# Rotary keys turned two pages at a time, sequences written out, and the sample states decayed on GpSimd

## The chip, the core and the metric

The kernel runs on one core of a Trainium2 chip. The metric is the device time of one launch in microseconds. The kernel before took 3429.12 us (median of three runs, 3422.21 to 3435.35). The engines are called PE (TensorE; its weight loads are listed as PEld), DVE (VectorE), ACT (ScalarE), POOL (GpSimd) and SP (SyncE, which issues DMAs).

## What is computed

One inference step of a two-layer trunk for a prompt of 256 tokens and for 8 sample sequences of 4 tokens. Each layer projects the normalized input once and feeds three branches, a Mamba-2 SSD, an RWKV-7 mixer and latent attention, merges them through gates, and adds a convolutional feed-forward part. Two pieces matter here.

Attention of the samples over 16 cached pages of 128 positions each. A key is the 128 features made from the latent by a weight, beside 64 rotary features shared by all heads:

```python
kn = jnp.einsum('blr,rhe->blhe', ckv, w_kb)
kp = jnp.broadcast_to(kpe[:, :, None, :], kn.shape[:-1] + (MLA_ROPE,))
k = rmsnorm(jnp.concatenate([kn, kp], axis=-1), k_norm_g)
sc = jnp.einsum('bqhe,blhe->bhql', q, k) * scale     # then a softmax over 2048 + 4 positions
```

The SSD recurrence, over two chunks of 128 for the prompt and one of 4 for each sample, from a given state:

```python
y_diag = einsum('bcgjls,bcsgjp->bclgjp', cb * exp(segsum(da)), xd)
states = einsum('bclgn,bcgjl,bclgjp->bcgjpn', bm, decay_to_end, xd)
h_next = h * exp(cs[..., -1]) + states
y_off  = einsum('bclgn,bcgjpn,bcgjl->bclgjp', cm, h_in, exp(cs))
```

## The kernel before, in words

The layers run in a loop of two turns. Inside, each stage is a block in which every engine has its own instruction list; semaphores order them, and a barrier of all engines closes the stage. The order of the work within an engine is the order in which the code is written; nothing plans it.

**cache_attention** (`def cache_attention`, L1091) works through 8 sequences of 16 pages. For each page PE turns the latents (two 128x128 transposes, L1224) and the rotary keys (one of 128x64, L1225) into `turn_bank`; ACT copies the latents to `ch` with rounding (L1305) and the rotary keys to `kpT` (L1306); DVE makes the rest `cl` (L1374). The keys then take 18 products of 352 columns (L1245: three parts of float32r, two halves of the rank, three bank groups), and one plain float32 product (L1249) adds the scores of the rotary part from 64 rows. ACT squares the keys (L1319), DVE sums them (L1388). While a sequence runs, the softmax and value steps of the one before are spread over its pages by `finish`: TURN_TOP and SPREAD (L1257, L1260) turn and spread the maximum. The turn of page j+1 is queued ahead of the keys of page j. `seqs` (L1152) writes out the first and the last sequence; the six between run in a loop of three turns, two sequences a turn, on PE, ACT and DVE. Beside it POOL runs the recurrence of the RWKV samples. SP issues the page loads.

**mla_absorb** (L963) runs before it and builds `qr`, the rotary part of the queries, with one DVE copy (L1035) that PE waits for, and ends with a chain on DVE and ACT that makes the scores of the new tokens.

**ssd_tiles** (L2518) follows the SSD projection. After the products inside the first prompt chunk (L2600), PE turns the 8 sample states (`turn_state`, L2619: 8 transposes a sequence into one of two bank pairs), ACT copies each to `seq_T` (L2771), and `read_states` (L2626) reads four at a time; `seq_T` has four slots, so the fifth copy waits for the first reading. Then come eight `update(b)` (16 products each, of 32 rows; on the helper's line L2571), the samples' own output (`inside(SAM)`, L2597 and L2603), the turn of the second chunk's x (`turn_x`, L2584), its four `segments` (one product of 512 columns each, L2571), its reading of the prompt state (`yo`), the new prompt state, `inside(1)` (L2600, L2606) and the turn of the prompt state (L2739), which ACT copies (L2776) and SP stores. DVE decays and adds each sample state in `add(b)`, eight instructions (L2826), and SP stores it. PE's list and DVE's list interleave the pieces so that the two bank pairs 0 to 3 and the banks 4 to 7 come free in time. The stage behind it is `merge`, whose first instruction on ACT is L1673.

Of the kernel before, what the change touches and what calls it, by code (L numbers as in the profile page):

```python
# [962 lines left out]
def mla_absorb(nc, k):  # L963


    with Stage(nc) as st:
# [9 lines left out]
        with st.block() as block:  # L976
# [6 lines left out]
            def _(pe):  # L983
# [22 lines left out]
                nc.tensor.matmul(banks[0:NSAM, 7, 0:256], k.kpe_rT[:, SEQ:T], k.qr[:, :, :].rearrange("p b c -> p (b c)"),  # L1006
# [18 lines left out]
            def _(dve):  # L1025
# [9 lines left out]
                nc.vector.tensor_copy(k.qr[:, :, :].rearrange("p b (h t) -> p h b t", h=HEADS),  # L1035
                                      k.qrT[:, :, SEQ:T].rearrange("p h (b t) -> p h b t", b=NB)).then_inc(qa_kept, 1)
# [54 lines left out]
def cache_attention(nc, k):  # L1091
# [19 lines left out]
    with Stage(nc) as st:  # L1111
# [16 lines left out]
        kpT = reuse(1344, 2, P)[0:ROPE, :, :]  # L1128
# [53 lines left out]
        with st.block() as block:  # L1182
# [33 lines left out]
            def _(pe):  # L1216
                def turn(b, slot, uses, j):
# [5 lines left out]
                    for r in range(2):  # L1223
                        nc.tensor.transpose(xbank[:, r * P:(r + 1) * P], lat[:, slot, j, r * P:(r + 1) * P], k.col("ident"))  # L1224
                    nc.tensor.transpose(xbank[0:ROPE, 2 * P:3 * P], kpe[:, slot, j, :], k.col("ident")).then_inc(turned, 1)  # L1225

                def body(b, slot, uses):
                    base = b * PAGES
                    pe.wait_ge(q_split, b + 1)
                    for j in range(PAGES):  # L1230
# [18 lines left out]
                        nc.tensor.matmul(kbank[:, bank, o:o + 32], kpT[:, x, :], k.qr[:, ds(b, 1), :].rearrange("p o c -> p (o c)"),  # L1249
# [40 lines left out]
            def _(act):  # L1290
# [8 lines left out]
                def head(b, j):  # L1299
# [5 lines left out]
                    nc.scalar.copy(ch[:, x, :], xbank[:, 0:2 * P])  # L1305
                    nc.scalar.copy(kpT[:, x, :], xbank[0:ROPE, 2 * P:3 * P]).then_inc(headed, 1)  # L1306
# [1211 lines left out]
def ssd_tiles(nc, k):  # L2518
# [8 lines left out]
    with Stage(nc) as st:  # L2527
# [24 lines left out]
        h_turned, h_kept, yo_made, y_scaled, y_made, y_read, skip_ready = (st.sem(n) for n in (  # L2552
            "state_turned", "state_kept", "y_from_state", "y_state_scaled", "y_made", "y_read", "skip_ready"))
        dcol_ready, c_zero, cm_ready, bm_ready = (st.sem(n) for n in ("skip_column", "c_cleared", "c_masked", "b_masked"))
        up_made, nat_ready, s_out, p_out = (st.sem(n) for n in ("update_made", "state_updated", "sample_states_stored", "prompt_state_stored"))
# [9 lines left out]
        with st.block() as block:  # L2565
            @block.tensor
            def _(pe):
# [42 lines left out]
                def turn_state(b):  # L2610
# [3 lines left out]
                    elif b == 1:  # L2614
                        pe.wait_ge(ssm_kept, 1)
                    else:
                        pe.wait_ge(h_kept, b - 1)
# [4 lines left out]
                def read_states(m):  # L2622
                    pe.wait_ge(h_kept, 4 * m + 4)
# [6 lines left out]
                def update(b):  # L2630
                    if b < 2:
                        pe.wait_ge(h_kept, 7 + b)
# [62 lines left out]
                for b in range(6):  # L2695
                    turn_state(b)
# [10 lines left out]
                pe.wait_ge(y_read, 1)  # L2707
# [4 lines left out]
                pe.wait_ge(steps_in_1, 2)  # L2712
                segments(1, 0, 5)
                update(3)
                pe.wait_ge(y_read, 2)
                segments(1, 1, 4)
                update(4)
                pe.wait_ge(m_exp, 6)
                segments(1, 2, 5)
                update(5)  # L2720
                pe.wait_ge(m_exp, 7)
                segments(1, 3, 4)
                pe.wait_ge(xdd_ready, 3)
                for g in range(2):
                    last = one(banks[:, 6 + g, :], k.xbcT[:, 10 + g, cols[1]], ssm_T[:, g * 512:(g + 1) * 512])
                last.then_inc(yo_made, 1)
                update(6)
                update(7)
                pe.wait_ge(nat_ready, 7)
                for g in range(2):  # L2730
# [301 lines left out]
```

## Time and profile before

| what | us |
|---|---|
| median of three runs | 3429.12 |
| the profiled execution | 3435.03 |
| its span | 3433.2 |
| PE busy (share of the span) | 2973.6 (87%) |
| DVE busy | 1851.0 (54%) |
| ACT busy | 1332.6 (39%) |
| POOL busy | 849.6 (25%) |
| mean granted PE clock | 0.917 |

A profile is one execution; its span is the time from the first instruction to the last, 1.8 us less than the execution's own time. An engine can be busy without being at its peak: matmuls are pipelined and their listed durations overlap, so the distance between two starts tells more than a duration. PEclk 1.00 is 2.4 GHz, 0.50 is 1.2 GHz. Cache attention lies at about 547 to 1080 us of the span in the first layer and at 2250 to 2790 us in the second; the ssd stage at 1181 to 1270 us and at 2884 to 2975 us.

### The profile page before, as it was taken

Reading aid. Unit: us, or ns where it says so; the run is one execution under the profiler, and the core shown is the slowest. Engines: PE = TensorE matmul, PEld = TensorE weight load, DVE = VectorE, ACT = ScalarE, POOL = GpSimd, SP = SyncE. Lnnn points to the kernel's source line nnn. Section 1 sums busy time; section 2 is a strip of 40 time slices with the busy share of each in tenths; the row PEclk is TensorE's granted clock in tenths of the full one; section 3 lists DMA queues with packets and bytes.
Section 4 is the critical chain, followed back from the end, with each engine's and each line's share of the span. In section 5 each row is a group of like instructions: output and inputs, shape, how many; then the busy total and the mean of one; then the engine's idle time right before and its main releaser. Section 6 shows DMA issues by size and latency. Waiting matters only on the chain. (4 is left out here: it accounts for less than half of the span.)

```text
span 3433.2 us, 67647 instructions
## 1 busy us (share of the span) xinstructions
PE 2973.6 (87%) x26688; PEld 2662.5 (78%) x26688; DVE 1851.0 (54%) x3191; ACT 1332.6 (39%) x2096; POOL 849.6 (25%) x688
## 2 busy tenths in 40 slices
PE   7659687999997879989986687789999978799898
PEld 6559546888886759989984685478888867599898
DVE  5563353555554745569455534545555537554793
ACT  3412343444443324344344123434444434233543
POOL 0041000699970100000001310007999501000000
PEclk9879888999998979999988898889999989699999
DMA  5100302211112336455450002021111132453654
GB/s 165 45 2 5 112 6 68 64 32 45 50 56 89 101 93 181 127 148 147 116 168 18 3 15 101 10 69 59 35 54 38 56 114 76 129 161 110 161 143 120
DMA packets 444034, 282.38 MB, mean 82 GB/s; under 512 B 64686, under 2 KB 439256, under 8 KB 443082
## 3 DMA queue, kind: packets, MB, share of 16 engines
q1 hardware_dynamic: 441492, 276.85, 28.5%
q8 instruction: 212, 3.47, 0.4%
q10 hardware_dynamic: 2232, 1.26, 0.2%
q14 instruction: 98, 0.80, 0.1%
HBM read 258.75 MB, written 19.29 MB: 81 GB/s over the span
## 5 line engine op out<-in xcount | busy, mean ns | idle before, releaser
L1245 PE MATMUL key_banks<-w_kb_head,latent_T_head 128*128 128x352 f32 x1536 | 519.0, 338 | 0.0
L1245 PE MATMUL key_banks<-w_kb_rest,latent_T_head 128*128 128x352 f32 x1536 | 496.9, 324 | 0.0
L1245 PE MATMUL key_banks<-w_kb_head,latent_T_rest 128*128 128x352 f32 x1536 | 496.5, 323 | 0.0
L290 DVE TENSOR_TENSOR w_rests<-w_ring,w_heads 128x2048 fp32r<-128x2048 f32 (+1 forms) x180 | 390.0, 2170 | 161.7 <-ACT w_heads L284 161.2
L284 ACT CAST w_heads<-w_ring 128x2048 fp32r<-128x2048 f32 (+1 forms) x180 | 325.6, 1812 | 60.4 <-DMA w_ring<-in_w_in_dram 22.8
L1065 POOL TENSOR_TENSOR rwkv_state_tmp<-rwkv_state,vec 128x1024 f32<-128x1024 f32 x64 | 153.5, 2398 | 681.7 <-DMA rwkv_state<-in_state_rwkv_dram 676.9
L1305 ACT CAST latent_T_head<-turn_bank 128x256 fp32r<-128x256 f32 x256 | 95.5, 373 | 558.4 <-PE turn_bank L1225 558.4
L1388 DVE TENSOR_REDUCE w_kb<-key_sq 128x8 f32<-128x1024 f32 x256 | 309.4, 1209 | 0.0
L1374 DVE TENSOR_TENSOR latent_T_rest<-turn_bank,latent_T_head 128x256 fp32r<-128x256 f32 x256 | 108.6, 424 | 363.3 <-ACT w_kb L1306 363.3
L1245 PEld LDWEIGHTS key_banks<-w_kb_rest,latent_T_head 128*128 128x128 f32 x1536 | 291.2, 190 | 0.0
L1245 PEld LDWEIGHTS key_banks<-w_kb_head,latent_T_head 128*128 128x128 f32 x1536 | 290.7, 189 | 0.1
L1245 PEld LDWEIGHTS key_banks<-w_kb_head,latent_T_rest 128*128 128x128 f32 x1536 | 290.1, 189 | 0.0
L1319 ACT ACTIVATE key_sq<-key_banks 128x1056 f32<-128x1056 f32 x256 | 269.2, 1052 | 8.7 <-PE key_banks L1249 8.7
L297 PE MATMUL ffn_banks<-h_heads_T,w_heads 128*128 128x288 f32 x704 | 211.6, 301 | 25.6 <-DVE h_rests_T L2041 22.3
L406 POOL TENSOR_TENSOR bonus_product<-fT 128x2304 f32<-128x2304 f32 x2 | 10.1, 5042 | 854.7 <-DVE fT L436 854.7
L298 PE MATMUL ffn_banks<-h_rests_T,w_heads 128*128 128x288 f32 x704 | 209.3, 297 | 0.0
L299 PE MATMUL ffn_banks<-h_heads_T,w_rests 128*128 128x288 f32 x704 | 208.6, 296 | 0.0
L1068 POOL TENSOR_TENSOR rwkv_state_tmp<-rwkv_state_tmp 128x512 f32<-128x512 f32 (+4 forms) x320 | 197.1, 616 | 25.1
L297 PEld LDWEIGHTS ffn_banks<-h_heads_T,w_heads 128*128 128x128 f32 x704 | 133.6, 190 | 29.2 <-DVE h_rests_T L2041 23.2
L297 PE MATMUL merge_banks<-out_heads,w_heads 128*128 128x288 f32 x512 | 151.6, 296 | 5.3 <-DVE out_rests L1713 5.3
L299 PE MATMUL merge_banks<-out_heads,w_rests 128*128 128x288 f32 x512 | 151.7, 296 | 0.0
L298 PE MATMUL merge_banks<-out_rests,w_heads 128*128 128x288 f32 x512 | 151.7, 296 | 0.0
(561 smaller groups left out, 7424.6 us busy)
## 6 DMA issues: line engine op xcount, KB each, us to landing
w_ring<-in_w_in_dram SPq DMA_DIRECT2D x48, 1024.0 KB, 5.4
w_ring<-in_ffn_w_up_dram SPq DMA_DIRECT2D x88, 512.0 KB, 4.9
latents<-in_cache_kv_latent_dram SPq DMA_DIRECT2D x256, 128.0 KB, 2.0
w_ring<-in_w_gate_dram SPq DMA_DIRECT2D x48, 512.0 KB, 3.9
w_ring<-in_ffn_w_down_dram SPq DMA_DIRECT2D x32, 384.0 KB, 3.3
w_ring<-in_ffn_w_down_dram SPq DMA_DIRECT2D x32, 320.0 KB, 3.8
rope_keys<-in_cache_k_rope_dram SPq DMA_DIRECT2D x256, 32.0 KB, 1.8
ssm_native<-in_state_ssm_dram SPq DMA_DIRECT2D x16, 512.0 KB, 7.2
```

The costliest lines, as they stand in the source:

```text
L284: nc.scalar.copy(heads[:, slot, 0:tiles * P], ring[:, slot, 0:tiles * P]).then_inc(rounded, 1)
L290: ops.tensor_tensor(rests[:, slot, 0:tiles * P], ring[:, slot, 0:tiles * P], heads[:, slot, 0:tiles * P].bitcast(F32), ALU.subtract).then_ ...
L297: nc.tensor.matmul(out, wh, xh, start=start, stop=False)
L298: nc.tensor.matmul(out, wh, xl, start=False, stop=False)
L299: return nc.tensor.matmul(out, wl, xh, start=False, stop=stop)
L1065: c(nc.gpsimd.tensor_tensor(tmp, S, over_v(n, t), ALU.mult))
L1068: c(nc.gpsimd.tensor_tensor(tmp[:, :, 0:w], tmp[:, :, 0:w], tmp[:, :, w:2 * w], ALU.add))
L1245: last = nc.tensor.matmul(kbank[:, 3 * x + n, 0:KB], c[:, x, r * P:(r + 1) * P], w[:, r, cols], start=r == 0 and m == 0, stop=r == 1 and m ...
L1305: nc.scalar.copy(ch[:, x, :], xbank[:, 0:2 * P])
L1319: nc.scalar.activation(sq[:, x, :], kbank[:, 3 * x:3 * x + 3, 0:KB], ACT.Square).then_inc(squared, 1)
L1374: nc.vector.tensor_tensor(cl[:, x, :], xbank[:, 0:2 * P], ch[:, x, :].bitcast(F32), ALU.subtract).then_inc(t_kept, 1)
L1388: nc.vector.tensor_reduce(ss[:, slot, j, :], sq[:, x, f:f + KW].rearrange("p (h e) -> p h e", e=NOPE), AX.X, ALU.add).then_inc(summed, 1)
```

## The change

In cache attention the rotary keys of an even page and the odd one behind it are turned by one 128x128 transpose, into a `kpT` of 128 rows, and copied once. The product with the queries now runs over all 128 rows for every page, with a `qr` of two halves that holds zeros in the rows of the other page; one copy and two memsets more on DVE build it in mla_absorb. All eight sequences are written out on PE, ACT and DVE; SP keeps its loop. In ssd_tiles the states are turned as before but copied by ACT (even) and DVE (odd); POOL multiplies each whole state by its decay after it is turned; `add(b)` is one DVE addition; the second chunk's x is turned early, its segments and the prompt's pieces are written in another order and in other banks, and the prompt state is turned before `inside(1)`.

```diff
@@ mla_absorb, vector
-                nc.vector.tensor_copy(k.qr[:, :, :].rearrange("p b (h t) -> p h b t", h=HEADS), ...)
+                for half in range(2):
+                    rows = slice(ROPE * half, ROPE * half + ROPE)
+                    last = nc.vector.tensor_copy(k.qr[rows, half, :, :].rearrange("p b (h t) -> p h b t", h=HEADS), ...)
+                last.then_inc(qa_kept, 1)
+                nc.vector.memset(k.qr[ROPE:P, 0, :, :], 0.0)
+                nc.vector.memset(k.qr[0:ROPE, 1, :, :], 0.0)
@@ cache_attention, seqs
-            body(0, 0, 0)
-            with eng.Fori(0, NB // 2 - 1) as i:
-                body(i * 2 + 1, 1, i)
-                body(i * 2 + 2, 0, i + 1)
-            body(LAST, 1, NB // 2 - 1)
+            for b in range(NB):
+                body(b, b % 2, b // 2)
@@ tensor
-                    nc.tensor.transpose(xbank[0:ROPE, 2 * P:3 * P], kpe[:, slot, j, :], k.col("ident")).then_inc(turned, 1)
+                    if j % 2 == 0:
+                        pair = kpe[:, slot, j:j + 2, :].rearrange("p j c -> p (j c)")
+                        nc.tensor.transpose(xbank[:, 2 * P:3 * P], pair, k.col("ident")).then_inc(turned, 1)
+                    else:
+                        last.then_inc(turned, 1)
...
-                        nc.tensor.matmul(kbank[:, bank, o:o + 32], kpT[:, x, :], k.qr[:, ds(b, 1), :]...
+                        nc.tensor.matmul(kbank[:, bank, o:o + 32], kpT[:, j // 2 % 2, :], k.qr[:, x, ds(b, 1), :]...
@@ scalar
-                    nc.scalar.copy(kpT[:, x, :], xbank[0:ROPE, 2 * P:3 * P]).then_inc(headed, 1)
+                    if x == 0:
+                        last = nc.scalar.copy(kpT[:, j // 2 % 2, :], xbank[:, 2 * P:3 * P])
+                    last.then_inc(headed, 1)
@@ ssd_tiles, tensor
-                for b in range(6):
+                turn_state(0)
+                turn_state(1)
+                pe.wait_ge(y_read, 1)
+                turn_x(1, 4)
+                for b in range(2, 6):
                     turn_state(b)
...
                 read_states(1)
+                pe.wait_ge(steps_in_1, 2)
+                pe.wait_ge(xdd_ready, 3)
+                segments(1, 0, 4)
+                segments(1, 1, 5)
                 pe.wait_ge(bm_ready, 1)
                 update(0)
                 update(1)
+                pe.wait_ge(m_exp, 6)
+                segments(1, 2, 4)
+                pe.wait_ge(m_exp, 7)
+                segments(1, 3, 5)
...
-                inside(SAM, 4, True)
-                turn_x(1, 6)
+                inside(SAM, 6, True)
...
@@ scalar
-                for b in range(NB):
+                for b in range(0, NB, 2):
...
@@ gpsimd
+                pool.wait_ge(e_ready, 2)
+                for b in range(NB):
+                    pool.wait_ge(h_turned, b + 1)
+                    nc.gpsimd.tensor_tensor(nat[:, b, :, :], nat[:, b, :, :], bc(dec[:, :, b], P), ALU.mult).then_inc(decayed, 1)
@@ vector
                 def add(b):
                     dve.wait_ge(up_made, b + 1)
-                    for t in range(DT):
-                        last = nc.vector.scalar_tensor_tensor(nat[:, b, t, :], nat[:, b, t, :], dec[:, t, b:b + 1], ...
+                    dve.wait_ge(decayed, b + 1)
...
+                    nc.vector.tensor_tensor(state, made, state, ALU.add).then_inc(nat_ready, 1)
+
+                def keep(b):
+                    dve.wait_ge(h_turned, b + 1)
+                    if b >= 4:
+                        dve.wait_ge(yo_made, 1)
+                    nc.vector.tensor_copy(seq_T[:, b % 4, :], wide(2)).then_inc(odd_kept, 1)
...
-                finish(0, 1)
-                scaled(SAM, 0, 2)
-                dve.wait_ge(e_ready, 2)
+                finish(0, 1, 4)
+                keep(1)
+                dve.wait_ge(x_turned, 3)
+                dve.wait_ge(s_made, 1)
+                weighted(xd[:, 0, :], 4, dt[:, 1, :])
+                weighted(xdd[:, 0, :], 4, dt_end[:, 1, :]).then_inc(xdd_ready, 1)
+                for b in (3, 5, 7):
+                    keep(b)
+                scaled(SAM, 0, 2, 6)
                 add(0)
                 add(1)
...
```

PE's list at the end of page 1 of cache attention, before: the last key products (L1245), the rotary product, the turn of page 3 and the first products of page 2.

```order
L1245 MATMUL key_banks<-w_kb_rest,latent_T_head 128x352
L1245 MATMUL key_banks<-w_kb_head,latent_T_rest 128x352
L1249 MATMUL key_banks<-qr,w_kb 128x32
L1224 MATMUL turn_bank<-const,latents 128x128 x2
L1225 MATMUL turn_bank<-const,rope_keys 64x128
L1245 MATMUL key_banks<-w_kb_head,latent_T_head 128x352
```

The same place in the changed kernel:

```order
L1251 MATMUL key_banks<-w_kb_rest,latent_T_head 128x352
L1251 MATMUL key_banks<-w_kb_head,latent_T_rest 128x352
L1255 MATMUL key_banks<-qr,w_kb 128x32
L1226 MATMUL turn_bank<-const,latents 128x128 x2
L1251 MATMUL key_banks<-w_kb_head,latent_T_head 128x352
L1251 MATMUL key_banks<-w_kb_rest,latent_T_head 128x352
```

The third transpose is gone on every odd page; on even ones it stays, with 128 columns in place of 64.

PE's list in the ssd stage from the products inside the first chunk on, before (`ssm_native` are the sample states, `ssm_T` their turned copies, `b_by_seq` marks the updates, `decay_matrix,const` the segments):

```order
L2600 MATMUL ssd_banks<-decay_matrix,x_dt 64x128 x16
L2619 MATMUL ssd_banks<-const,ssm_native 128x128 x48
L2626 MATMUL ssd_banks<-ssm_T,samT 32x512 x8
L2619 MATMUL ssd_banks<-const,ssm_native 128x128 x16
L2626 MATMUL ssd_banks<-ssm_T,samT 32x512 x8
L2571 MATMUL ssd_banks<-b_by_seq,x_dt_decayed 128x128 x16
```

and in the changed kernel:

```order
L2608 MATMUL ssd_banks<-decay_matrix,x_dt 64x128 x16
L2627 MATMUL ssd_banks<-const,ssm_native 128x128 x16
L2592 MATMUL ssd_banks<-const,xbcT 128x128 x8
L2627 MATMUL ssd_banks<-const,ssm_native 128x128 x32
L2635 MATMUL ssd_banks<-ssm_T,samT 32x512 x8
L2627 MATMUL ssd_banks<-const,ssm_native 128x128 x16
L2635 MATMUL ssd_banks<-ssm_T,samT 32x512 x8
L2579 MATMUL ssd_banks<-decay_matrix,const 128x512 x2
L2579 MATMUL ssd_banks<-b_by_seq,x_dt_decayed 128x128 x16
L2579 MATMUL ssd_banks<-decay_matrix,const 128x512 x2
```

The turn of x stands among the states, and all four segments of the second chunk stand in pairs around the first two updates.

PE's list at the end of the stage, before, from `update(5)` on (`prompt_ssm_T,xbcT` reads the prompt state, `x_dt_decayed,b_tm` makes the new one):

```order
L2571 MATMUL ssd_banks<-b_by_seq,x_dt_decayed 128x128 x8
L2571 MATMUL ssd_banks<-decay_matrix,const 128x512
L2571 MATMUL ssd_banks<-prompt_ssm_T,xbcT 128x512 x2
L2571 MATMUL ssd_banks<-b_by_seq,x_dt_decayed 128x128 x16
L2571 MATMUL ssd_banks<-x_dt_decayed,b_tm 128x512 x2
L2600 MATMUL ssd_banks<-decay_matrix,x_dt 64x128 x2
L2606 MATMUL ssd_banks<-const,ssm_T 128x128
```

and in the changed kernel, from `update(2)` on:

```order
L2579 MATMUL ssd_banks<-b_by_seq,x_dt_decayed 128x128 x16
L2579 MATMUL ssd_banks<-prompt_ssm_T,xbcT 128x512 x2
L2579 MATMUL ssd_banks<-b_by_seq,x_dt_decayed 128x128 x16
L2579 MATMUL ssd_banks<-x_dt_decayed,b_tm 128x512 x2
L2579 MATMUL ssd_banks<-b_by_seq,x_dt_decayed 128x128 x16
L2746 MATMUL ssd_banks<-const,prompt_ssm_T 128x128 x8
L2608 MATMUL ssd_banks<-decay_matrix,x_dt 64x128 x2
L2614 MATMUL ssd_banks<-const,ssm_T 128x128
```

The turn of the prompt state (L2746) has moved ahead of the products inside the chunk, which now end PE's list.

## Rows read from the trace of the kernel before

**Rows 1.** The stretches: length, busy us by engine, PEclk, DMA share, GB/s.

```profile
560.00:580.00 20.00, 20.00 (x127) 18.69 (x126) 9.21 (x17) 8.80 (x18) 0.00 (x0) 1.00 0.32 91
1221.00:1244.00 23.00, 23.00 (x112) 15.20 (x109) 14.61 (x45) 2.39 (x4) 0.00 (x0) 0.50 0.37 115
1245.00:1251.00 6.00, 3.40 (x36) 2.29 (x35) 5.23 (x16) 0.00 (x0) 0.00 (x0) 1.00 0.17 53
```

**Rows 2.** Timeline of weight loads, one page: start us, us, what, idle before.

```profile
706.18 0.29 PEld L1249 LDWEIGHTS key_banks<-qr,w_kb 64*128 64x128 f32 x2 [0.22 <-issue]
706.52 0.20 PEld L1224 LDWEIGHTS turn_bank<-const,latents 128*128 128x128 f32 x2
706.68 0.11 PEld L1225 LDWEIGHTS turn_bank<-const,rope_keys 128*64 128x64 f32 x1
```

**Rows 3.** The same page boundary, ACT and PE.

```profile
702.48 0.40 PE L1260 MATMUL misc_bank<-w_kb,const 32*128 32x32 f32 x2 [0.24 <-ACT w_kb L1344]
703.67 0.26 ACT L1306 COPY w_kb<-turn_bank 64x128 f32<-64x128 f32 x1
```

**Rows 4.** PE, first product of rotary keys of some pages, both layers.

```profile
614.45 0.40 PE L1249 MATMUL key_banks<-qr,w_kb 64*128 x2
1002.75 0.41 PE L1249 MATMUL key_banks<-qr,w_kb 64*128 64x32 f32 x2
1062.91 0.29 PE L1249 MATMUL key_banks<-qr,w_kb 64*128 64x32 f32 x1
2318.89 0.29 PE L1249 MATMUL key_banks<-qr,w_kb 64*128 x1
2706.43 0.41 PE L1249 MATMUL key_banks<-qr,w_kb 64*128 64x32 f32 x2
```

**Rows 5.** DVE in the absorb stage and at the start of the next.

```profile
531.54 0.28 DVE L1035 COPY qr<-qrT 64x256 f32<-64x256 f32 x1
538.28 0.29 DVE L1356 COPY new_c_and_one<-new_c 128x256 f32<-128x256 f32 x1 [1.40 <-PEq L228]
```

**Rows 6.** PE, plain float32 products of 128 and of 64 rows.

```profile
487.69 0.79 PE L858 MATMUL attn_banks<-knT,qnT 128*128 128x128 f32 x2
488.41 0.79 PE L859 MATMUL attn_banks<-krT,qrT 64*128 64x128 f32 x2
489.14 1.22 PE L858 MATMUL attn_banks<-knT,qnT 128*128 128x256 f32 x2
```

**Rows 7.** PE in the ssd stage of the first layer.

```profile
1202.46 1.96 PE L2619 MATMUL ssd_banks<-const,ssm_native 128*128 128x128 f32 x16
1208.92 1.92 PE L2626 MATMUL ssd_banks<-ssm_T,samT 128*32 128x512 f32 x16
1217.07 2.05 PE L2571 MATMUL ssd_banks<-b_by_seq,x_dt_decayed 32*128 32x128 f32 x32
1227.01 2.08 PE L2571 MATMUL ssd_banks<-b_by_seq,x_dt_decayed 32*128 32x128 f32 x16
1229.02 2.08 PE L2571 MATMUL ssd_banks<-decay_matrix,const 128*128 128x512 f32 x2
1252.78 0.70 PE L2600 MATMUL ssd_banks<-decay_matrix,x_dt 128*64 128x128 f32 x4
1263.47 1.91 PE L2739 MATMUL ssd_banks<-const,prompt_ssm_T 128*128 128x128 f32 x8
```

**Rows 8.** The other engines in and behind the ssd stage.

```profile
1190.70 3.75 POOL L2791 TENSOR_TENSOR decay_matrix<-const,dt_a 128x1024 f32<-128x1024 f32 x2
1191.39 1.26 DVE L2855 TENSOR_TENSOR dt_to_end<-dt,exp_sums 128x48 f32<-128x48 f32 x1
1252.95 1.22 DVE L2893 TENSOR_TENSOR prompt_ssm_T<-prompt_ssm_T,ssd_banks 128x1024 f32<-128x1024 f32 x1 [0.60 <-PE ssd_banks L2571]
1265.42 1.01 ACT L2776 COPY x_dt<-ssd_banks 128x1024 f32<-128x1024 f32 x1 [21.65 <-PE ssd_banks L2739]
1270.73 2.22 ACT L1673 ACTIVATE merged<-ssd_yT 128x1152 f32<-128x1152 f32 x2 [4.30 <-PEq L228]
```

More of the change, by code:

```diff
@@ L1005, in _ @@
                                      start=r == 0, stop=False)
[L1006 removed]
+                nc.tensor.matmul(banks[0:NSAM, 7, 0:256], k.kpe_rT[:, SEQ:T], k.qr[0:ROPE, 0, :, :].rearrange("p b c -> p (b c)"),
                                  start=False, stop=True).then_inc(new_made, 1)
@@ L1034, in _ @@
                                           banks[:, 4, r * 256:(r + 1) * 256].rearrange("p (h b t) -> p h b t", h=HEADS, b=NB)).then_inc(qa_kept, 1)
-                nc.vector.tensor_copy(k.qr[:, :, :].rearrange("p b (h t) -> p h b t", h=HEADS),
-                                      k.qrT[:, :, SEQ:T].rearrange("p h (b t) -> p h b t", b=NB)).then_inc(qa_kept, 1)
+                for half in range(2):
+                    rows = slice(ROPE * half, ROPE * half + ROPE)
+                    last = nc.vector.tensor_copy(k.qr[rows, half, :, :].rearrange("p b (h t) -> p h b t", h=HEADS),
+                                                 k.qrT[:, :, SEQ:T].rearrange("p h (b t) -> p h b t", b=NB))
+                last.then_inc(qa_kept, 1)
+                nc.vector.memset(k.qr[ROPE:P, 0, :, :], 0.0)
+                nc.vector.memset(k.qr[0:ROPE, 1, :, :], 0.0)
                 dve.wait_ge(squared, 2)
@@ L1248, in body @@
                         bank, o = score_place(x, slot)
-                        nc.tensor.matmul(kbank[:, bank, o:o + 32], kpT[:, x, :], k.qr[:, ds(b, 1), :].rearrange("p o c -> p (o c)"),
+                        nc.tensor.matmul(kbank[:, bank, o:o + 32], kpT[:, j // 2 % 2, :], k.qr[:, x, ds(b, 1), :].rearrange("p o c -> p (o c)"),
                                          start=False, stop=True, skip_group_check=True).then_inc(scored, 1)
@@ L1304, in head @@
                         act.wait_ge(scored, b * PAGES + (j - 1))
-                    nc.scalar.copy(ch[:, x, :], xbank[:, 0:2 * P])
-                    nc.scalar.copy(kpT[:, x, :], xbank[0:ROPE, 2 * P:3 * P]).then_inc(headed, 1)
+                    last = nc.scalar.copy(ch[:, x, :], xbank[:, 0:2 * P])
+                    if x == 0:
+                        last = nc.scalar.copy(kpT[:, j // 2 % 2, :], xbank[:, 2 * P:3 * P])
+                    last.then_inc(headed, 1)
                 def body(b, slot, uses):
@@ L2714, in _ @@
                 update(3)
-                pe.wait_ge(y_read, 2)
-                segments(1, 1, 4)
+                pe.wait_ge(m_exp, 9)
+                for g in range(2):
+                    last = one(banks[:, 4 + g, :], k.xbcT[:, 10 + g, cols[1]], ssm_T[:, g * 512:(g + 1) * 512])
+                last.then_inc(yo_made, 1)
                 update(4)
-                pe.wait_ge(m_exp, 6)
-                segments(1, 2, 5)
                 update(5)
-                pe.wait_ge(m_exp, 7)
-                segments(1, 3, 4)
@@ L2723, in _ @@
-                pe.wait_ge(xdd_ready, 3)
+                pe.wait_ge(y_scaled, 2)
                 for g in range(2):
-                    last = one(banks[:, 6 + g, :], k.xbcT[:, 10 + g, cols[1]], ssm_T[:, g * 512:(g + 1) * 512])
-                last.then_inc(yo_made, 1)
+                    last = one(banks[:, 4 + g, :], b_tm[:, 1, g, :], xdd[:, 0, g * 512:(g + 1) * 512])
+                last.then_inc(s_made, 1)
                 update(6)
                 update(7)
-                pe.wait_ge(nat_ready, 7)
@@ L2730, in _ @@
-                for g in range(2):
-                    last = one(banks[:, g, :], b_tm[:, 1, g, :], xdd[:, 0, g * 512:(g + 1) * 512])
-                last.then_inc(s_made, 1)
-                pe.wait_ge(m_ready, 3)
-                pe.wait_ge(y_scaled, 2)
-                inside(1, 4, True)
-                pe.wait_ge(nat_ready, 8)
                 pe.wait_ge(ssm_ready, 1)
                 for t in range(DT):
-                    last = nc.tensor.transpose(banks[:, 2 + t // 4, t % 4 * P:(t % 4 + 1) * P], ssm_T[:, block_of(t)], ident)
+                    last = nc.tensor.transpose(banks[:, 4 + t // 4, t % 4 * P:(t % 4 + 1) * P], ssm_T[:, block_of(t)], ident)
@@ L2740, in _ @@
                 last.then_inc(ssm_turned, 1)
+                pe.wait_ge(m_ready, 3)
+                pe.wait_ge(y_read, 2)
+                inside(1, 6, True)
             @block.scalar
@@ L2770, in _ @@
                         act.wait_ge(yo_made, 1)
-                    nc.scalar.copy(seq_T[:, b % 4, :], wide(2 * (b % 2))).then_inc(h_kept, 1)
+                    nc.scalar.copy(seq_T[:, b % 4, :], wide(0)).then_inc(even_kept, 1)
                 for q in range(4):
                     act.wait_ge(seg_made, 6 + q)
-                    decays(1, q, (5, 4)[q % 2])
+                    decays(1, q, 4 + q % 2)
                 act.wait_ge(ssm_turned, 1)
-                nc.scalar.copy(xd[:, 0, :], wide(2)).then_inc(p_kept, 1)
+                nc.scalar.copy(xdd[:, 0, :], wide(4)).then_inc(p_kept, 1)
             @block.gpsimd
```

60 lines of the change are left out of this document (26 added, 34 removed).

## Prediction

> **What bounds the kernel now.** I read the busy times first: PE leads every other engine by far, so a change counts where it shortens PE's list, PE's waits, or the end of a stage. I then went to the two stages that change. In cache attention PE is busy for all of 20 us out of 20 at the full clock, with DVE and ACT under half [rows 1]; each page costs what PE's instructions cost. The timeline of one page boundary shows the pieces: the rotary product loads its weights twice from 706.18 on, the two latent turns follow at 706.52, the rotary turn at 706.68 [rows 2]. The ssd stage is another matter. PE is busy for 23.00 of 23 us there, yet at the granted clock 0.50, which is 1.2 GHz [rows 1]; it had fallen after the updates and the small sample products, and eight updates of 32 rows, segments and more passed before it rose. Between 1245 and 1251 us it stood at 1.00. So this stage is bound by PE's list and by how much of it is granted 2.4 GHz.
>
> **Cache attention, transposes.** There are 256 pages in the two layers, and half of them lose the rotary turn: 128 transposes. The price is a distance between starts on PE. Two latent turns take 706.68 - 706.52 = 0.16, so 0.08 each, and the rotary load itself lasts 0.11 [rows 2]. I take 0.09: 128 x 0.09 = 11.5 us. The 128 turns that stay load 128 columns instead of 64; the latent turns already load 128 in 0.08, so I add nothing. Bounds: 10 us (0.08 each), and 15 us by the state transposes of the ssd stage, 16 in 1.96 us there, which is 0.12 each [rows 7]; below, if the wider load showed by 0.03 on the other 128, the gain would be 8.
>
> **Rotary product over 128 rows.** Twice the rows, the same columns. In prompt attention a plain float32 product of 128 rows starts at 487.69 and the next, of 64 rows and as many columns, at 488.41; that one's successor starts at 489.14: 0.72 and 0.73 [rows 6]. Cost nothing, and the idle 0.22 us before its weights [rows 2] stays.
>
> **The copy of the keys.** ACT drops 128 copies of 0.26 us [rows 3]. ACT waits for PE on every page and has the time, so this is hidden, but for one place: PE waits 0.24 us for the spread of the maximum on ACT [rows 3], once for each of the 14 sequences with a successor. The chain to it runs through the ACT head of page 7, an odd one, on DVE and back. It comes 0.26 earlier, so the 0.24 go: 14 x 0.24 = 3.4 us. Bounds 0 and 3.4. Turning the maximum, one page earlier, hangs on page 6, which keeps its copy; nothing there.
>
> **Writing out the sequences.** The last sequence is written out already: 1062.91 - 1002.75 = 60.16 us for 15 pages [rows 4], and with a sixteenth of 3.7 and the 0.28 for the turn that its last page lacks, 64.1. The six of the loop take 1002.75 - 614.45 = 388.3 in the first layer and 2706.43 - 2318.89 = 387.5 in the second [rows 4], against 6 x 64.1 = 384.8. The excess, 3.5 and 2.7, sits at the loop's turns, where PE stands still about 1 us. I take all of it: 6.2 us. Bounds 0 (the same waits, elsewhere) and 6.2.
>
> **The absorb stage.** One more copy of 0.28 us [rows 5] stands in front of PE's products, and two memsets of about as much stand in front of the DVE sum that ends the stage: 0.84 a layer, +1.7 us. Bounds 0.6 and 2.2. Cache attention together: -11.5 - 3.4 - 6.2 + 1.7 = -19.4 us.
>
> **The ssd stage, reading the states.** Times of the first layer. Inside the first chunk PE ends at 1202.46, and the two readings end at 1217.07, where the updates start [rows 7]. In the new order: the first state is turned by 1203.4 (16 transposes in 1.96, so 0.95 a state [rows 7]). POOL then decays it. The nearest rows for that multiply of 128x1024 are two of POOL in 3.75, so 1.87 each [rows 8]; it runs to 1205.3. DVE's product with silu z reads two tiles of SBUF. Another such DVE instruction, on only 48 columns, took 1.26 us and ended at 1192.65, just behind the end of POOL's first product, 1190.70 + 1.87 = 1192.57 [rows 8]: it had waited for POOL. So the product here starts at 1205.3, not 1203.9, and ends at 1206.5 with 1.22 us, as DVE's row of 1024 columns has it [rows 8]. DVE's copy of state 1 follows to 1207.7, the two weighted tiles of the second chunk to 1210.1, the copy of state 3 to 1211.3; PE turns state 5 by 1212.4, reads (1.9 [rows 7]) by 1214.3; copy 5, turn 7 and copy 7 lead to 1218.7 and the second reading to 1220.7. That is 3.6 us later than before, with the second chunk's x turned and weighted meanwhile.
>
> The Trainium skill ("SBUF — State Buffer", section Who interferes with whom) says that a VectorE instruction with two SBUF inputs and a GpSimd instruction that reads SBUF exclude each other for the whole instruction, and that one with at most one SBUF input does not. The trace agrees with the first half. By the second, DVE's copies out of PSUM do not wait for the eight decays; if they did, four waits of up to 1.87 would add 7 us a layer.
>
> **From there to the end.** Two segments, two updates and two segments at the full clock are six pieces of 1.0 us at the full clock (2.05 for two updates; for a segment half of its 2.01, the distance to the next start at the low clock, as 1227.01 to 1229.02 for an update and the duration of 2.08 of both [rows 7]): 1226.7. The samples' own products took 1227.01 - 1219.1 less 1.9 for the turn of x, 6.0, and the clock fell in them, as I expect again: 1232.7. Then at 1.2 GHz six updates at 2.01, 12.1; two products as long as two segments each, 8.0; the turn of the prompt state 1.9 (a row of 1.91); the products inside the chunk 1263.47 - 1252.78 = 10.7 [rows 7]. PE ends at 1265.4, DVE's last two at 1267.9. Before, ACT's copy ended at 1266.43, the store followed, and the next stage's ACT began at 1270.73, 4.30 later [rows 8]. Now the store has long been sent, and a boundary without one costs about the 1.40 us by which DVE stood idle at the start of cache attention [rows 5]: 1269.3. That is 1.4 us earlier at the low clock throughout. Before, at least 6 us from 1245 on were granted 1.00, 2.6 of them idle on PE [rows 1]. If the new order gets one such stretch and fills it, that does the work of 12 us at the low clock, 6 more saved: 7.4. I take the middle, 4.5 us a layer: -9. Bounds: 1.4 and, with the clock up all through, the 17 of the first rival. DVE's shorter additions and the bank waits save PE little, since at 1.2 GHz PE is last.
>
> **The sum.** -19.4 - 9 = -28.4 us on 3435.03, the profiled execution's own time (its span and 1.8 around it): 3406.6. The median of the runs lies 5.9 lower, so 3400.7; I say 3401.
>
> **Rivals.**
> The clock stays at 1.00 in the ssd stage. For it: dense segments now stand in pairs, and PE has no idle stretch after 1221. Against: 23 busy us at 0.50 [rows 1]. Then the 32.7 us of updates, products and turn behind the samples' own part halve to 16.4, PE ends near 1249 and the stage near 1253: 17 us a layer, 34 in place of 9, so 3376. The Trainium skill ("TensorE: Matmul & The Clock Gate", section Part 1) says that the half clock is the state of an idle engine and that sustained matmul work releases it; by that rule this is the likely case, and the time 3376. The trace does not bear it out, with its 23 us.
>
> The clock falls already while the states are read, since DVE's and ACT's copies leave PE more idle than before. Against: it stayed up through such gaps. The two readings, the turns and the six pieces after them, some 11 us of PE's work behind 1210, then take twice as long: +22 on the forecast, 3423.
>
> PE gains nothing from the shorter turns, because ACT's and DVE's part sets the page: the 11.5 fall away, 3412. Against: PE is busy 20.00 of 20 us [rows 1].
>
> The rotary weights load ahead now that all rows are used, as key weights do: 256 x 0.22 = 56 us more, 3345. Against: the products of 128 rows start no sooner [rows 6].
>
> Slower: the written-out code reaches PE too slowly. 192 pages ran from the loop. At 1 us, the price of a loop turn, for every third page, +64 + 6 (nothing is saved at the turns), so 3471. It decides from (28 + 17) / 192 = 0.23 us a page. Against: the 16 pages of the last sequence, written out, run at 3.7 to 4.7 us without one such stall.
>
> **How the numbers follow.** Forecast 0.52; clock up 0.14; clock down early 0.12; turns for nothing 0.11; weights ahead 0.04; slow code 0.07. Within 0.5% (17 us, about what this kernel's measurement can tell) lie the early fall of the clock, half of the turns' case and a little of the forecast: 0.21. Faster 0.72, slower 0.07. The range, 3368 to 3428, takes in the first four cases with the bounds of the terms.
>
> **What would show it.** Right: pages end 0.09 us sooner on average on every second one and no page of 1 us more at a loop's turn; PE's wait for the spread gone; PE's second reading of states ends 3 to 4 us later after the first chunk's products, with a DVE product of over 2 us in between; the next stage starts 1.5 to 9 us sooner. Wrong: full clock over the ssd stage's second half; no idle before the rotary weights; pages of even length over 3.7 us; the stage longer than 89 us.

## The result and the profile after

The changed kernel takes 3340.27 us (median of four runs, 3336.11 to 3341.19), the kernel before beside it 3429.88 (3422.21 to 3435.35): a ratio of 0.974, 95% interval 0.9719 to 0.9761. The forecast was 3401 with a range of 3368 to 3428, so the gain was three times as large as forecast: 89 us, not 28. The profiled execution took 3339.95 us, 95.1 less than that of before.

First, where the 95.1 us went, as distances between starts in the two traces. The three rows add up to 97.5 us; the other stages together run 2.4 longer.

| stretch | before, layers 1 and 2 | after | difference |
|---|---|---|---|
| cache attention, first page's rotary product to the last page's | 507.58, 506.86 | 466.27, 466.53 | -81.6 |
| ssd stage, first turn of a state to ACT's start in the next stage | 68.27, 69.22 | 60.38, 60.36 | -16.8 |
| absorb stage, its first product to the first rotary product | 33.75, 33.44 | 34.03, 34.06 | +0.9 |

So it is mostly cache attention. The first and last page in the timeline of PE, both layers, first of before (the last page of its first layer is 1062.91 in [rows 4]), then of after:

```profile
555.33 0.41 PE L1249 MATMUL key_banks<-qr,w_kb 64*128 64x32 f32 x2
...
2259.76 0.41 PE L1249 MATMUL key_banks<-qr,w_kb 64*128 64x32 f32 x2
...
2766.62 0.41 PE L1249 MATMUL key_banks<-qr,w_kb 64*128 64x32 f32 x2
```

```profile
556.00 0.30 PE L1255 MATMUL key_banks<-qr,w_kb 128*128 128x32 f32 x2
...
1022.27 0.30 PE L1255 MATMUL key_banks<-qr,w_kb 128*128 128x32 f32 x2
...
2214.94 0.30 PE L1255 MATMUL key_banks<-qr,w_kb 128*128 128x32 f32 x2
...
2681.47 0.30 PE L1255 MATMUL key_banks<-qr,w_kb 128*128 128x32 f32 x2
```

The timeline of weight loads at one page boundary, which answers to [rows 2]:

```profile
734.37 0.19 PEld L1251 LDWEIGHTS key_banks<-w_kb_head,latent_T_rest 128*128 128x128 f32 x1
734.53 0.35 PEld L1255 LDWEIGHTS key_banks<-qr,w_kb 128*128 128x128 f32 x2
734.72 0.28 PEld L1226 LDWEIGHTS turn_bank<-const,latents 128*128 128x128 f32 x2
734.97 0.14 PEld L1229 LDWEIGHTS turn_bank<-const,rope_keys 128*128 128x128 f32 x1
735.08 0.19 PEld L1251 LDWEIGHTS key_banks<-w_kb_head,latent_T_head 128*128 128x128 f32 x1
```

The load of the rotary product follows the last key load after 0.16 us, in step with the key loads, and no idle time stands behind its row. Before there was 0.22 us of it [rows 2]. The groups of weight loads give the sum, first of before, then of after (busy us and mean ns, then the idle time ahead of them and what ended it):

```profile
L1249 PEld LDWEIGHTS key_banks<-qr,w_kb 64*128 64x128 f32 x512 | 75.3, 184 | 56.3 <-issue 56.3
```

```profile
L1255 PEld LDWEIGHTS key_banks<-qr,w_kb 128*128 128x128 f32 x512 | 88.9, 188 | 0.0
```

A load of 128 rows lasts no longer than one of 64 (188 and 184 ns), but it no longer stands idle first. That is the rival "the rotary weights load ahead", with its 56 us and its 3345.

The stretches of the changed kernel, which answer to [rows 1]: cache attention, and four of the first layer's ssd stage.

```profile
560.00:580.00 20.00, 20.00 (x137) 20.00 (x136) 10.45 (x18) 8.45 (x16) 0.00 (x0) 1.00 0.35 98
1181.00:1190.00 9.00, 9.00 (x81) 6.12 (x80) 4.20 (x5) 2.39 (x4) 0.00 (x0) 1.00 0.39 118
1191.00:1197.00 6.00, 6.00 (x35) 4.34 (x34) 4.13 (x5) 0.00 (x0) 0.00 (x0) 0.50 0.28 88
1198.00:1203.00 5.00, 4.89 (x52) 3.34 (x52) 4.59 (x5) 0.00 (x0) 0.00 (x0) 1.00 0.29 93
1205.00:1219.00 14.00, 14.00 (x70) 9.06 (x68) 1.62 (x2) 1.01 (x1) 0.00 (x0) 0.50 0.50 151
```

In cache attention PE was busy for 20.00 of 20 us before as well; what changed is the column of weight loads, 18.69 then and 20.00 now, and 137 products in place of 127. In the ssd stage PE worked at 1.2 GHz for about 7 and 15 us, where it had been about 24 and 13.

PE's timeline of that ssd stage, which answers to [rows 7]:

```profile
1161.98 1.97 PE L2627 MATMUL ssd_banks<-const,ssm_native 128*128 128x128 f32 x16
...
1167.50 1.94 PE L2627 MATMUL ssd_banks<-const,ssm_native 128*128 128x128 f32 x16 [1.81 <-DVE ssm_T L2848]
...
1180.29 1.98 PE L2579 MATMUL ssd_banks<-decay_matrix,const 128*128 128x512 f32 x4
...
1186.10 0.30 PE L2605 MATMUL ssd_banks<-decay_matrix_sample,x_dt 32*64 32x32 f32 x4
...
1190.67 3.78 PE L2579 MATMUL ssd_banks<-b_by_seq,x_dt_decayed 32*128 32x128 f32 x32
1194.39 3.51 PE L2579 MATMUL ssd_banks<-prompt_ssm_T,xbcT 128*128 128x512 f32 x4
1197.83 2.05 PE L2579 MATMUL ssd_banks<-b_by_seq,x_dt_decayed 32*128 32x128 f32 x32
...
1208.22 0.70 PE L2608 MATMUL ssd_banks<-decay_matrix,x_dt 128*64 128x128 f32 x4
```

The second reading ends at 1180.29, 18.3 us behind the first chunk's products (before: 14.6). Two updates take 3.72 us at half the clock and 1.98 at all of it. The other engines there, which answer to [rows 8], each from its own timeline:

```profile
1163.22 12.25 POOL L2810 TENSOR_TENSOR ssm_native<-ssm_native,state_decay 128x1024 f32<-128x1024 f32 x6 [5.53 <-PE ssd_banks L2627]
```

```profile
1163.42 2.79 DVE L2828 TENSOR_TENSOR ssd_yT<-ssd_yT,silu_zT 128x1024 f32<-128x1024 f32 x1
1166.14 1.21 DVE L2848 COPY ssm_T<-ssd_banks 128x1024 f32<-128x1024 f32 x1
...
1220.41 1.22 DVE L2828 TENSOR_TENSOR ssd_yT<-ssd_yT,silu_zT 128x1024 f32<-128x1024 f32 x1
```

```profile
1208.33 1.01 ACT L2786 COPY x_dt_decayed<-ssd_banks 128x1024 f32<-128x1024 f32 x1 [21.52 <-PE ssd_banks L2746]
1222.36 2.22 ACT L1681 ACTIVATE merged<-ssd_yT 128x1152 f32<-128x1152 f32 x2 [13.02 <-PEq L228]
```

DVE ends at 1221.63 and the next stage's ACT starts 0.73 us later; the copy that the store waits for was done 13 us before.

### The profile page after: what moved, and what is told of

Same layout as the page of the kernel before. It is cut to its first block and busy times, and to the rows that moved or that the text cites. A ratio compares the mean times of both kernels' runs of the same rounds, so it can differ in the third digit from the quotient of the medians.

```text
span 3338.1 us, 66365 instructions
## 1 busy us (share of the span) xinstructions
PE 2876.3 (86%) x26560; PEld 2636.4 (79%) x26560; DVE 1849.3 (55%) x3093; ACT 1308.2 (39%) x1960; POOL 882.4 (26%) x704
## 3 DMA queue, kind: packets, MB, share of 16 engines
q8 instruction: 200, 3.28, 0.4%
```

## The experiments

All ratios are to the kernel before, run beside it on the same chip. In e1 and e2 two theories stood against each other: A, that weights of 64 rows are not loaded beside a running product of 128 rows; B, that the gain lay in the transposes, the copies or the written-out code. The later experiments have theories A, B and C of their own, each named in the text of what was expected.

**e1, the 128 rows alone.** On the kernel before, with `qr` made for 128 rows (the main lines of the edit):

```diff
-        kpT = reuse(1344, 2, P)[0:ROPE, :, :]
+        kpT = reuse(1344, 2, P)
-                    nc.scalar.copy(kpT[:, x, :], xbank[0:ROPE, 2 * P:3 * P]).then_inc(headed, 1)
+                    nc.scalar.copy(kpT[0:ROPE, x, :], xbank[0:ROPE, 2 * P:3 * P]).then_inc(headed, 1)
+                nc.vector.memset(k.qr[ROPE:P, :, :], 0.0)
```

> The kernel before with one thing changed: the product of the rotary keys runs over 128 rows (the rows 64 to 127 of the queries hold zeros, the turns stay 64 columns wide and one a page). Theory A, the weights of a 64-row product are not loaded beside a running 128-row product, those of a 128-row product are: the idle before these weights (56.3 us summed over 512 loads) goes, and most of the 81.6 us that cache attention lost in the changed kernel with it, less 14 for the 128 transposes and 6 for the written-out sequences: about 60 us less than before, 3370, between 3360 and 3380. Theory B, the gain came from the transposes, the copies or the written-out code: no change, 3430, and the idle of 0.22 us before the weights stays.

Measured: 3372.74 us, ratio 0.9833 (0.9803 to 0.9863). Cache attention runs 477.69 and 478.45 us, 58.3 less than before, and a plain page takes 3.38 to 3.40 us in place of 3.69 to 3.71. Theory A. The zeros do no work, and yet this one edit is two thirds of the whole gain. A plain page gained 0.31 us, more than the idle 0.22: the latent turn's first load, which came 0.34 us behind the first rotary one (706.18 and 706.52 in [rows 2]), now comes 0.19 behind it. Pages with softmax or value work between the two gained less.

**e2, 64 rows again.** On the changed kernel:

```diff
-kpT[:, j // 2 % 2, :], k.qr[:, x, ds(b, 1), :]
+kpT[ROPE * x:ROPE * x + ROPE, j // 2 % 2, :], k.qr[ROPE * x:ROPE * x + ROPE, x, ds(b, 1), :]
```

> The changed kernel with the product of the rotary keys over 64 rows again (rows 0 to 63 for an even page, 64 to 127 for an odd one), the keys still turned in pairs. Theory A: the idle of 0.22 us returns before each pair of weight loads, and the kernel takes some 60 us more than the changed one, about 3400, which is what had been forecast. Theory B: as the changed kernel, 3340. A third case: only one of the two row halves pays, then 3370, with the idle on even or on odd pages alone.

Measured: 3403.73 us, ratio 0.9899 (0.9867 to 0.9931). The group of its loads:

```profile
L1255 PEld LDWEIGHTS key_banks<-qr,w_kb 64*128 64x128 f32 x512 | 75.4, 184 | 56.2 <-issue 56.2
```

Theory A again; even and odd pages stand idle alike, 0.22 us each in the timeline, so it doesn't matter which half of the rows it is. This kernel is what the forecast had described, a changed kernel whose rotary product gains nothing. It is 35 us faster than the kernel before it (24 to 46), where the forecast had 28.

**e6, 96 rows.** As e1, with `kpT[0:96, x, :]` and `k.qr[0:96, ds(b, 1), :]`.

> The kernel with the rotary product over 128 rows alone, now over 96 (rows 64 to 95 of the queries hold zeros). Theory A1, weights load ahead where the next product has as many rows as the running one: the idle is back, 56 us summed, and the time is that of before, 3430. Theory A2, 96 rows count as the whole array, as 128 do: no idle and 3372, as with 128.

Measured: 3376.15 us, ratio 0.9837 (0.9806 to 0.9869), as with 128 rows. Its loads:

```profile
L1250 PEld LDWEIGHTS key_banks<-qr,w_kb 96*128 96x128 f32 x512 | 89.3, 189 | 0.0
```

So the condition is not that two neighbours have equally many rows: 96 behind 128 load ahead, 64 behind 128 do not.

**e7, two halves of 64 rows.** On the kernel before:

```diff
+                        for c0 in (0, 16):
+                            last = nc.tensor.matmul(kbank[:, bank, o + c0:o + c0 + 16], kpT[:, x, :], k.qr[:, ds(b, 1), c0:c0 + 16]...
```

> The kernel before with the rotary product of cache attention, still over 64 rows, cut into two of 16 columns with the same weights. Theory A, the idle of 0.22 us belongs to the switch from 128 to 64 rows: it stays once a page (56 us summed), and the second product costs its own two loads alone, 0.15 to 0.34 us a page as its first one does from start to next start: 3470 to 3520. Theory B, each 64-row product has its own idle: 0.56 a page, 3570, and the idle of these loads sums to over 100 us.

Measured: 3477.14 us, ratio 1.0124 (1.0106 to 1.0141); cache attention 530.32 and 530.29 us, 46 more than before, or 0.18 us for each second product.

```profile
L1250 PEld LDWEIGHTS key_banks<-qr,w_kb 64*128 64x128 f32 x1024 | 132.4, 186 | 56.0 <-issue 56.0
```

Theory A: twice the loads, the same idle time. It belongs to the step from 128 rows to 64, not to a product of 64 rows as such. The added product stands behind one of 16 columns alone, which might be too short to show a wait. Prompt attention settles that: a product over 64 rows and 256 columns loads its weights twice, and the two loads follow within 0.50 us without idle time between them, although the first part of the product is running by then (486.89 in the last fence of this document).

**e5, prompt attention over 128 rows too.** The forecast had leaned on prompt attention, where a 128-row and a 64-row product alternate and look alike [rows 6]. On the changed kernel, `qrT` and `krT` get 128 rows and

```diff
+                nc.vector.memset(k.qrT[ROPE:P, :, :], 0.0)
+                nc.vector.memset(k.krT[ROPE:P, :, :], 0.0)
```

> The changed kernel once more, as the base for the runs beside it: 0.974 of the kernel before.

> The changed kernel with the rotary product of prompt attention (L859) over 128 rows as well: qrT and krT get 128 rows, the lower 64 set to zero by two memsets on DVE. In the changed kernel the weight loads of L859 stand idle for 9.1 us and those of L858, the 128-row product that alternates with it, for 6.0. Theory A, a switch between 64 and 128 rows keeps weights from loading ahead in both directions (which is why the two products looked alike in the rows that the forecast used): both idles shrink, 8 to 12 us less. Theory A2, only the step from 128 to 64 rows pays: 4 to 8 us less. Theory B, plain float32 products of 128 columns behind one another have this idle whatever their rows: nothing, and the memsets cost up to 4 us.

Measured: the changed kernel 3346.38 us, ratio 0.9748 (0.9734 to 0.9762); with this edit 3326.71, ratio 0.9702 (0.9683 to 0.9721). The groups of weight loads in that stage, of the changed kernel run beside it and with the edit:

```profile
L858 PEld LDWEIGHTS attn_banks<-knT,qnT 128*128 128x128 f32 x64 | 11.9, 232 | 6.1 <-issue 4.6
L859 PEld LDWEIGHTS attn_banks<-krT,qrT 64*128 64x128 f32 x64 | 11.3, 221 | 9.3 <-issue 8.1
L866 PEld LDWEIGHTS attn_banks<-const,samT 128*32 128x32 f32 x96 | 9.0, 103 | 6.1 <-issue 4.6
L875 PEld LDWEIGHTS attn_banks<-const,scores 128*128 128x128 f32 x48 | 5.4, 141 | 5.4 <-DVE scores L949 4.8
```

```profile
L861 PEld LDWEIGHTS attn_banks<-krT,qrT 128*128 128x128 f32 x64 | 12.2, 212 | 1.1
L860 PEld LDWEIGHTS attn_banks<-knT,qnT 128*128 128x128 f32 x64 | 11.3, 217 | 2.6 <-issue 2.2
L868 PEld LDWEIGHTS attn_banks<-const,samT 128*32 128x32 f32 x96 | 9.3, 97 | 2.6
L877 PEld LDWEIGHTS attn_banks<-const,scores 128*128 128x128 f32 x48 | 6.0, 160 | 10.9 <-DVE scores L951 10.9
```

Theory A, and it explains the misleading rows: behind a product of 64 rows the 128-row load stood idle too, so the two products looked alike because both paid. 15.2 us of idle time go and 5.5 come back as a wait for DVE; the stage shortens by 9.8 us over both layers (from the first L858 to the first product of the absorb stage: 38.14 and 37.58 us, then 33.02 and 32.93). Part of these 9.8 us is the clock and not the idle time alone: 1.2 GHz was granted for 10 to 11 us of the stage in the changed kernel and for 6.5 with the edit, where it rose about 3 us after the first product. At the same clock the gain is seen by itself: from one attention head's products to the next's, 3.72 us became 2.70 at 1.2 GHz (the first head) and 3.87 became 3.28 at 2.4 GHz (the last four). The memsets (3.7 us a layer on DVE) cost nothing: the stage in which they run keeps its 76.5 us. The two profiled executions lie 21.4 us apart. Besides the 9.8, another 6.1 are clock in the first layer's ssd stage, which took 54.02 us there and 60.07 in the run beside it; the last 5.5 are spread over the other stages and not explained. Measured twice, the ratio is 0.004 lower, 14 us. This version beats both kernels.

**e9, fewer switches in the RWKV preparation.** There two products of 64 rows, in the two halves of the rows, run side by side, and one of 128 rows follows. On e5, every second tile has the order g, w, a:

```diff
+                    for part in (decay_and_a, gate) if d % 2 == 0 else (gate, decay_and_a):
+                        part()
```

> The kernel with both rotary products over 128 rows once more, as the base for the run beside it: 0.970 of the kernel before.

> The kernel with both rotary products over 128 rows, and in the preparation of the RWKV branch the order of PE's products turned on every second tile: w, a, g, then g, w, a (w and a are two products of 64 rows that run side by side in the two halves of the rows, g is one of 128). Each switch of rows stands idle for 0.39 us at the full clock and 0.76 at half of it there; 8 of 16 a layer go. Theory A, PE bounds this stretch: 16 x 0.39 = 6 us less, up to 9. Theory B, ACT, which takes four results a tile, bounds it as soon as PE is faster: 0 to 2 us.

Measured: e5 again 3333.24 us, ratio 0.9706 (0.9681 to 0.973); with the edit 3333.10, ratio 0.9708 (0.9684 to 0.9733). Theory B. The loads of the 128-row product, in e5 again and with the edit:

```profile
L358 PEld LDWEIGHTS prep_banks<-fT,g_up 128*128 128x128 f32 x32 | 6.4, 250 | 9.8 <-issue 9.8
```

```profile
L362 PEld LDWEIGHTS prep_banks<-fT,g_up 128*128 128x128 f32 x32 | 5.9, 221 | 9.3 <-ACT sam_gate L388 4.9 <-issue 3.8
```

The switches are fewer, but PE now waits for ACT. From its first of these products to the first one behind them this stretch took 13.2 us in both layers, against 13.1 in the changed kernel with the old order and about as much 1.2 GHz (4 us); the 16.0 us of e5 again have 11 us at 1.2 GHz in them.

**e3, the loop put back** around six sequences of the changed kernel.

> The changed kernel with the loop of three turns put back around six sequences on PE, ACT and DVE. Theory A, the loop's turns cost what the excess over a written-out sequence said (3.5 and 2.7 us): 6 us more than the changed kernel, 3346. Theory B, this excess was waits that a written-out sequence has too: within 2 us of the changed kernel. Theory C, the written-out code gives more than the turns (the fetch of instructions within the loop is slower too): 10 us or more.

Measured: 3351.38 us, ratio 0.9763 (0.974 to 0.9786), 0.15 to 0.23% above the changed kernel in its two measurements, 5 to 8 us, no more than the interval, so the traces have to decide. There cache attention takes 469.42 and 470.03 us, 6.7 more than the changed kernel's. Theory A.

**e4, the old ssd stage in the changed kernel, and e8, the new one in the kernel before.**

> The changed kernel with the ssd stage of the kernel before. Theory A, the stage gained what the first layer's trace shows, 68.3 to 60.4 us from the first chunk's products to the next stage, in both layers: 16 us more than the changed kernel, 3356. Theory B, as forecast, 4.5 a layer: 3349. Theory C, part of the gain lies in how the store or the clock meets the next stage and is given back there: under 5 us.

> The kernel before with the new ssd stage alone. The same old stage took 68.3, 69.2, 63.9, 62.4, 68.3 and 62.4 us in six layers of three traces, the new one 60.4, 60.4, 61.5, 60.4, 54.1 and 60.3. Theory A, the clock in the stage decides and averages out over runs: 6 us a layer, 12 in all. Theory B, the faster stage is partly given back behind it, as the difference of 5 to 7 us between the changed kernel and the one with the old stage says: 5 to 7 us less than before. Theory C, the forecast: 9.

Measured: e4 3347.42 us, ratio 0.9754 (0.9731 to 0.9776); e8 3426.88, ratio 0.9976 (0.9964 to 0.9989), which is 8.2 us (3.8 to 12.4). For e8 this is nearest to C, the forecast's 9, and its interval takes in B's 5 to 7 and just A's 12. For e4 the interval of the ratio holds the changed kernel's own, so it bounds the loss to somewhere between nothing and 12 us. The traces show why single pairs mislead: the same old stage took 62.4 to 69.2 us in ten layers of five traces, the new one 59.8 to 61.5 in thirteen layers and 54.0 to 54.1 in three, of eight traces. The means, 65.7 and 59.2, differ by 6.5 a layer, 13 in all, more than the timed gain. Some of it is given back behind the stage: the stretch from the next stage to the absorb stage of the second layer took 953.9 to 960.4 us behind the old stage (mean 956.8) and 956.5 to 964.6 behind the new one (mean 960.4), in the traces with the prompt attention of before. What causes that is open.

**e10, the decays later.** On the changed kernel, POOL waits for `odd_kept` before its first decay:

```diff
+                pool.wait_ge(odd_kept, 1)
```

> The changed kernel with POOL's decays in the ssd stage held back until DVE has copied the first odd state. Theory A, DVE's product with silu z had waited for POOL's first decay: it takes 1.2 us in place of 2.79, and the second reading of states ends 1.5 us sooner after the first chunk's products (16.8 us behind them in place of 18.3); the run is 0 to 3 us faster, as far as the clock lets it through. Theory B, the 2.79 us come of something else: the product stays at 2.8. Theory C: the later decays hold up the additions of DVE, and the run is slower.

Measured: 3344.29 us, ratio 0.9749 (0.9724 to 0.9775), no change that can be told from nothing. DVE's timeline:

```profile
1165.17 1.23 DVE L2829 TENSOR_TENSOR ssd_yT<-ssd_yT,silu_zT 128x1024 f32<-128x1024 f32 x1
1166.32 1.22 DVE L2849 COPY ssm_T<-ssd_banks 128x1024 f32<-128x1024 f32 x1
```

The product takes 1.23 us in place of 2.79, and the second reading ends 1180.47 - 1163.73 = 16.7 us behind the first chunk's products, as expected. The stage shortens by 0.5 and 0.4 us alone: the first stretch at 1.2 GHz behind it lasted some 10 us in place of 7. In the changed kernel DVE's copy out of PSUM had started at 1166.14 and taken 1.21 us while POOL's decays ran. Both halves of the Trainium skill's rule that the forecast used ("SBUF — State Buffer", section Who interferes with whom) agree with that: the product with two SBUF inputs waited for POOL's instruction, the copy without one did not.

## Why the prediction was wrong, step by step

**The failed step** is the one on the rotary product over 128 rows: "Cost nothing, and the idle 0.22 us before its weights [rows 2] stays." It went, and with it 58.3 us (e1), against 56.3 of idle time listed ahead of these loads. "No idle before the rotary weights" was among the forecast's own signs of being wrong. The reasoning took two starts in prompt attention, 0.72 and 0.73 us apart, as proof that the number of rows is indifferent [rows 6]. They could not prove that. In that place each product stands behind one with the other number of rows, so both pay (e5). A comparison that could have shown it needs a 128-row product behind a 128-row one, and the key products next to the rotary one were that: they load every 0.16 us without idle time. The rival was named with the right price, 56 us and 3345; its chance, 0.04, was set by that one misread pair.

The Trainium skill ("TensorE: Matmul & The Clock Gate", section Step-by-step: what each phase is for) says that a load is pulled ahead of running products where the row groups don't conflict or where it goes to the background buffer, and that its time depends on columns, not on rows. The load's own duration agrees (184 and 188 ns); that it is hidden or not does depend on the rows here, with 0.22 us of idle time for 64 rows and none for 96 and 128.

**Transposes**, 11.5 forecast. Between e1 and e3, which differ in cache attention by the turn in pairs alone, the traces show 8.3 and 8.4 us, 16.7 with the copies. With 64 rows (e2) all of the stage's gain is 22.9, less 6.7 for the loop and 2.1 to 3.4 for the wait below: 12.8 to 14.1, or 0.10 to 0.11 a transpose where 0.09 was taken. Right within its bounds.

**The copy of the keys**, 3.4 forecast. In e2 PE's idle time ahead of the spread, 4.8 us over both layers before, fell to 2.7, of which the profile puts 1.4 down to ACT: 2.1 to 3.4 gained, by how one counts. In the changed kernel it is 5.5, and the wait for the turn of the maximum rose from 24.5 to 28.7 (in e1 they are 7.6 and 26.5), because the pages of PE are shorter while the chain on DVE and ACT is not:

```profile
L1263 PE MATMUL misc_bank<-const,w_kb 128*32 128x128 f32 x16 | 4.8, 298 | 28.7 <-DVE w_kb L1419 28.7
L1266 PE MATMUL misc_bank<-w_kb,const 32*128 32x32 f32 x32 | 6.9, 297 | 5.5 <-ACT w_kb L1352 5.5
```

**Writing out the sequences**, 6.2 forecast, 6.7 in the traces (e3). Right, and no page of 1 us more is left at a turn. **The absorb stage**, 1.7 forecast, 0.9 in the traces, inside its bounds.

**The ssd stage**, 9 forecast, 8.2 timed (e8). The reading of the states ended 3.7 us later where 3.6 had been worked out, with a DVE product of 2.79 us where "over 2" had been expected. Two sizes inside were off: the samples' own products took 4.57 us (1186.10 to 1190.67) in place of 6.0, since the clock fell only at their end, and the boundary 0.73 in place of 1.40. The one stretch at full clock from 1197 on came, for which the forecast had 7.4 us a layer; in the two traces the layers gained 7.9 and 8.9. The middle value of 4.5 fits the timed total, but the way to it, some given back behind the stage, was not foreseen.

So five of six terms held, the one for the copy with 64 rows alone, and e2 shows their sum: 35 us (24 to 46) against 28. That its median, 3404, lies so near 3401 is partly luck, since the kernel before ran 5 us slower beside it. The sixth term was put at zero and was worth twice the rest.

## What to carry to other kernels

Look at the idle time ahead of the weight loads by group, not only at PE's busy time: PE was listed as busy for 20.00 of 20 us while each plain page lost 0.3 us. Where products over 64 rows stand between products over 128, fill the operands up with zero rows (96 were enough here), or put the short ones next to each other (e7 shows no idle time between them; e9 shows that it gains nothing where another engine bounds the stretch). And before a row is taken to show that two forms cost the same, check what stands in front of each of them, since the cost may lie in the change from one to the other.

## What the runs showed of the hardware

- Weights of 64 rows behind a running product of 128 rows stand idle 0.22 us each time (512 loads in pairs, 256 idle times, 56.3 us); weights of 96 or 128 rows there do not (0.0). 64 rows behind 64 rows add none (e7, and the pairs of loads below).
- The idle time grows with what the running product still has to do: in prompt attention it was 0.22 us behind 128 columns and 0.65 behind 256 at 1.2 GHz, and 0.33 behind 256 at 2.4 GHz, in both directions of the switch. This fits a load that waits for the running product's end; only the switch itself was tested.

```profile
485.01 0.50 PEld L859 LDWEIGHTS attn_banks<-krT,qrT 64*128 64x128 f32 x2 [0.22 <-issue]
485.74 0.50 PEld L858 LDWEIGHTS attn_banks<-knT,qnT 128*128 128x128 f32 x2 [0.22 <-issue]
486.89 0.50 PEld L859 LDWEIGHTS attn_banks<-krT,qrT 64*128 64x128 f32 x2 [0.65 <-issue]
488.04 0.50 PEld L858 LDWEIGHTS attn_banks<-knT,qnT 128*128 128x128 f32 x2 [0.65 <-issue]
...
495.21 0.29 PEld L859 LDWEIGHTS attn_banks<-krT,qrT 64*128 64x128 f32 x2 [0.33 <-issue]
495.84 0.77 PEld L866 LDWEIGHTS attn_banks<-const,samT 128*32 128x32 f32 x8 [0.33 <-issue]
```

- One and the same ssd code took 62.4 to 69.2 us, by how long its stretches at 1.2 GHz were: 40 us of them in the first layer before, which took 68.3, and 27 in the second layer of e4, which took 62.4. A pair of traces is too little to size a change in such a stage.
